# State-space stage: matrices fetched ahead, inputs one block later, another order of the gate matmuls

## What is computed

```python
u = (h @ w_in).reshape(B, S, G, C)          # 64 groups of 16 channels
# x[s] = a * x[s-1] + Bbar u[s], complex, 64 states a group
y = einsum('bsgp,gcp->bsgc', xr, c_re) - einsum('bsgp,gcp->bsgc', xi, c_im) + d_skip * u
y = gelu(y)
val, gate = split(y @ w_glu, 2)
h = h + val * sigmoid(gate)
```

## Time and profile before

| what | us |
|---|---|
| median of 3 runs | 1158.1 (1156.81 to 1161.51) |
| the profiled execution | 1160.05 |
| its span, first to last instruction | 1158.2 |
| PE busy | 1122.9 (97%) |
| DVE busy | 790.0 (68%) |
| ACT busy | 476.3 (41%) |
| POOL busy | 99.5 (9%) |

### The profile page before, as it was taken

One profiled execution on the slowest core, in us unless ns is written; L12 is line 12 of the kernel. 1 busy time (PEld: TensorE's weight loads), 2 busy tenths in 40 slices (PEclk: granted clock), 3 DMA queues, 4 the chain that ended last, 5 costly groups with the idle time before them and its releaser, 6 DMA issues.

```text
span 1158.2 us, 14812 instructions
## 1 busy us (share of the span) xinstructions
PE 1122.9 (97%) x5654; PEld 919.9 (79%) x5654; DVE 790.0 (68%) x1172; ACT 476.3 (41%) x718; POOL 99.5 (9%) x194
## 2 busy tenths in 40 slices
PE   9998999999999999999999979999999999999995
PEld 6776778788888888888778877887888888888874
DVE  6757758898776887678768855547764467635764
ACT  6455544345423543335452214334442244413431
POOL 3270008910000000000000000000000000000000
PEclk9999899899999999999999979999999999999998
DMA  6221103233343333433257853332232232233221
GB/s 225 87 69 37 37 19 109 74 109 111 110 137 117 109 128 103 134 110 123 97 173 216 234 162 108 94 108 91 92 104 96 91 101 100 91 99 102 82 82 72
DMA packets 61942, 125.68 MB, mean 109 GB/s; under 512 B 21808, under 2 KB 30512, under 8 KB 61872
## 3 DMA queue, kind: packets, MB, share of 16 engines
q1 hardware_dynamic: 60720, 120.54, 32.6%
q0 software_dynamic: 1152, 4.19, 1.0%
HBM read 110.04 MB, written 14.68 MB: 108 GB/s over the span
## 4 chain that ended last, share of the span: by engine, by line
PE 86%; DVE 6%; DMA 3%; issue 2%; ACT 2%; DVEq 1%; SPq 0%; ACTq 0%
PE bank L1418 27%; PE bank L1420 26%; PE bank L1419 26%; DMA ud_scratch<-UB 2%; DVE MX L1006 1%; DVE WL L812 1%; DVE P L1014 1%; PE bank L1745 1%; PE bank L1737 1%; ACT WH L477 1%; PE bank L1696 1%; PE bank L1437 1%; DMA yd_scratch<-Y 1%; DVEq L1005 1%; PE bank L1432 1%
## 5 line engine op out<-in xcount | busy, mean ns | idle before, releaser
L477 ACT ACTIVATE WH<-RAW 128x1024 fp32r<-128x1024 f32 (+1 forms) x184 | 190.1, 1034 | 387.7 <-PE bank L1420 367.8
L1418 PE MATMUL bank<-GH,WH 128*128 128x512 f32 x816 | 323.2, 396 | 4.2 <-DVE GL L1048 3.1
L1419 PE MATMUL bank<-GL,WH 128*128 128x512 f32 x816 | 318.8, 391 | 0.0
L1420 PE MATMUL bank<-GH,WL 128*128 128x512 f32 x816 | 318.7, 391 | 0.0
L812 DVE TENSOR_TENSOR WL<-RAW,WH 128x1024 fp32r<-128x1024 f32 (+1 forms) x184 | 221.2, 1203 | 46.9 <-ACT WH L477 46.2
L1418 PE MATMUL bank<-AH,WH 128*128 128x512 f32 x596 | 235.9, 396 | 2.7 <-DVE AL L1157 1.6
L1420 PE MATMUL bank<-AH,WL 128*128 128x512 f32 x596 | 232.9, 391 | 0.0
L1419 PE MATMUL bank<-AL,WH 128*128 128x512 f32 x596 | 232.7, 390 | 0.0
L1418 PEld LDWEIGHTS bank<-GH,WH 128*128 128x128 f32 x816 | 153.9, 189 | 38.9 <-DVE GL L1048 4.0
L1419 PEld LDWEIGHTS bank<-GL,WH 128*128 128x128 f32 x816 | 153.9, 189 | 32.8 <-issue 1.4
L1420 PEld LDWEIGHTS bank<-GH,WL 128*128 128x128 f32 x816 | 153.9, 189 | 32.6
(11 more groups left out here) (254 smaller groups left out, 997.0 us busy)
## 6 DMA issues: line engine op xcount, KB each, us to landing
RAW<-in_w_up SPq DMA_DIRECT2D x88, 512.0 KB, 3.4
RAW<-in_w_dn SPq DMA_DIRECT2D x32, 512.0 KB, 3.5
RAW<-in_w_glu SPq DMA_DIRECT2D x16, 512.0 KB, 3.6
RAW<-in_w_dn SPq DMA_DIRECT2D x16, 384.0 KB, 3.0
RAW<-in_w_wo SPq DMA_DIRECT2D x8, 512.0 KB, 3.5
od_scratch<-OO SPq DMA_DIRECT2D x8, 512.0 KB, 3.0
kd_scratch<-KT SPq DMA_DIRECT2D x8, 512.0 KB, 4.8
O<-od_scratch POOLq DMA_DIRECT2D x8, 512.0 KB, 5.3
```

What stands on the lines that cost most here:

```text
L477: act_(WH[b % RH][:, :n], RAW[b % RW][:, :n], ACT.Copy).then_inc(s_hi, 1)
L1418: mm(out, wh, hi_[:, k, :], start=start, stop=False)
L1419: mm(out, wh, lo_[:, k, :], start=False, stop=False)
L1420: return mm(out, wl, hi_[:, k, :], start=False, stop=stop)
```

## The change

TM and O get five places instead of two: tiles 0 and 4 lie in AH and AL at tiles 6 and 7, tile 3 in AH and AL at tiles 4 and 5, tile 7 where ET of tiles 0 and 1 was, tiles 1 and 5 and tiles 2 and 6 in the two old places. Tiles 0 to 3 are fetched before the stage's first waits, 4 to 7 during it, each when what lay in its place has been used. There is a fourth U buffer (over SQ1). Inputs and outputs come one block later: TensorE does block t, inputs(t - 3), outputs(t - 4), and VectorE and ScalarE follow. On SP the read of y stands behind the next u_out instead of behind its own write. The first three gate blocks all come behind the last outputs, in an order in which block 0 ends first, then 1, then 2.

```diff
+        matrices_at("_y6", ah_at + 6 * 4 * S, al_at + 6 * 4 * S, (0, 4))
+        matrices_at("_y4", ah_at + 4 * 4 * S, al_at + 4 * 4 * S, (3,))
+        matrices_at("_et", A0, A0 + 4096, (7,))
+        at = matrices_at("0", at, at + 4096, (1, 5))
+        at = matrices_at("1", at, at + 4096, (2, 6))
...
+        U2[3], _ = place("U23", [P, 2 * QJ, NK], F32, sq1_at)
...
+                if b == FIRST["dn02"] + 2:
+                    sp.wait_ge(s_mm, nth(FIRST["up02"] - 1))
+                    lags_in(0)
+                if b == FIRST["dn02"] + 4:
+                    sp.wait_ge(s_act, TILE0["h02"] + THIRDS[2][1])
+                    lags_in(1)
+                if b == FIRST["dn02"] + 6:
+                    lags_in(2)
...
             def u_in(j):
-                if j >= 3:
-                    sp.wait_ge(s_Y, j - 2)
+                if j >= 4:
+                    sp.wait_ge(s_Y, j - 3)
                 sp.wait_ge(s_uw, 16 * (j + 1))
...
-            for t in range(NJ + 3):
+            sp.wait_ge(s_mm, nth(FIRST["win"] - 1))
+            lags_in(3)
+            for t in range(NJ + 4):
                 if t < NJ:
                     load(FIRST["win"] + 4 + t)
                     u_out(t)
+                if 5 <= t <= NJ:
+                    y_in(t - 5)
+                if t < NJ:
                     u_in(t)
-                if t >= 3:
-                    y_out(t - 3)
-                    if t - 1 < NJ:
-                        lags_in(t - 1)
-                    y_in(t - 3)
+                if t == 5:
+                    sp.wait_ge(s_Y, 1)
+                    lags_in(4)
+                if t == 6:
+                    sp.wait_ge(s_Y, 2)
+                    lags_in(5)
+                    sp.wait_ge(s_E, 2)
+                    lags_in(7)
+                if t == 7:
+                    sp.wait_ge(s_Y, 3)
+                    lags_in(6)
+                if t >= 4:
+                    y_out(t - 4)
+                if t >= NJ:
+                    y_in(t - 4)
...
# VectorE (ScalarE likewise: gelu(t - 4), decay(t - 2), y_tile(t - 5))
-            for t in range(NJ + 4):
+            for t in range(NJ + 5):
                 if t < NJ:
                     u_out(t)
-                if 2 <= t < NJ + 2:
-                    states(t - 2)
-                if t >= 4:
-                    y_lo(t - 4)
+                if 3 <= t < NJ + 3:
+                    states(t - 3)
+                if t >= 5:
+                    y_lo(t - 5)
...
# POOL: fetch(0) and fetch(1) while the last third of the MLP runs, then
+            fetch(2)
+            pool.wait_ge(s_mm, nth(FIRST["win"] - 1))
+            fetch(3)
+            pool.wait_ge(s_Y, 1)
+            fetch(4)
+            pool.wait_ge(s_Y, 2)
+            fetch(5)
+            pool.wait_ge(s_E, 2)
+            fetch(7)
+            pool.wait_ge(s_Y, 3)
+            fetch(6)
...
# TensorE
             for t in range(2, NJ):
                 whole(FIRST["win"] + t, KD, GH, GL)
-                inputs(t - 2)
                 if t >= 3:
-                    outputs(t - 3)
-            inputs(NJ - 2)
-            outputs(NJ - 3)
-            inputs(NJ - 1)
-            outputs(NJ - 2)
-            glu_part((0, 1), range(0, 4))
+                    inputs(t - 3)
+                if t >= 4:
+                    outputs(t - 4)
+            for j in range(NJ - 3, NJ):
+                inputs(j)
+                outputs(j - 1)
             outputs(NJ - 1)
-            glu_part((0, 1), (4, 5))
-            glu_part((2,), range(0, 6))
-            glu_part((0, 1, 2), (6,))
-            glu_part((0, 1, 2), (7,))
+            glu_part((0,), range(0, 5))
+            glu_part((1,), range(0, 5))
+            glu_part((2,), range(0, 3))
+            glu_part((0, 1), (5,))
+            glu_part((2,), (3, 4))
+            glu_part((0,), (6, 7))
+            glu_part((1,), (6, 7))
+            glu_part((2,), range(5, 8))
```

More of the change, by code:

```diff
@@ L295, in build, with matrices_at @@
         KT, at = place("KT", [P, LQ, C * LQ], F32, at)
-        TM, O2, U2, XR, XI, UB, Y2, YB, RT = ([None, None] for _ in range(9))
-        U2 = [None] * 3
+        XR, XI, UB, Y2, YB, RT = ([None, None] for _ in range(6))
+        U2 = [None] * 4
+        TM, O2 = [None] * NJ, [None] * NJ
         at = f0
-        for i in range(2):
-            TM[i], at = place(f"TM{i}", [P, 2 * QJ, C * LQ], F32, at)
-            O2[i], at = place(f"O2{i}", [P, 2, QJ, C * LQ], F32, at)
+        ah_at, al_at = g_at + 2 * 4 * KD * S, g_at + 3 * 4 * KD * S
+        def matrices_at(name, tm_at, o_at, tiles):
+            tm, _ = place("TM" + name, [P, 2 * QJ, C * LQ], F32, tm_at)
+            o2, end = place("O2" + name, [P, 2, QJ, C * LQ], F32, o_at)
+            for j in tiles:
+                TM[j], O2[j] = tm, o2
+            return end
+        matrices_at("_y6", ah_at + 6 * 4 * S, al_at + 6 * 4 * S, (0, 4))
[3 more added lines that the diff above has]
+        at = matrices_at("1", at, at + 4096, (2, 6))
         for i in range(3):
             U2[i], at = place(f"U2{i}", [P, 2 * QJ, NK], F32, at)
+        U2[3], _ = place("U23", [P, 2 * QJ, NK], F32, sq1_at)
         for i in range(2):
@@ L344, in build @@
         s_kp, s_k0, s_kt, s_kw, s_ow = sem("KP"), sem("K0"), sem("KT"), sem("kd_written"), sem("od_written")
-        s_tmr, s_or = [sem("TM0"), sem("TM1")], [sem("O0"), sem("O1")]
-        s_uw, s_ur = sem("ud_written"), [sem(f"U{i}_loaded") for i in range(3)]
+        s_tmr = [sem(f"TM_of_tile{j}") for j in range(NJ)]
+        s_or = [sem(f"O_of_tile{j}") for j in range(NJ)]
+        s_uw, s_ur = sem("ud_written"), [sem(f"U{i}_loaded") for i in range(4)]
         s_rt, s_E, s_X, s_Y, s_g = sem("RT"), sem("E"), sem("states"), sem("Y"), sem("gelu")
@@ L402, in lags, with lags_in @@
                 sp.dma_start(KD_[j], KT[:]).then_inc(s_kw, 16)
+            def lags_in(j):
+                k = KD_[j]
+                sp.wait_ge(s_kw, 16 * (j + 1))
+                sp.dma_start(TM[j][:], bass.AP(k.tensor, k.offset, [[C * LQ, P], [C * LQ * P, GJ], [1, C * LQ]])
+                             ).then_inc(s_tmr[j], 16)
             for b in range(4, FIRST["win"] + 4):
@@ L782, in _ @@
                     hi(FIRST["win"] + t + RH)
[L783 to L786, removed]
-                if t >= 4:
-                    y_tile(t - 4)
+                if 4 <= t < NJ + 4:
+                    gelu(t - 4)
+                if 4 <= t < NJ + 2:
+                    decay(t - 2)
+                if t >= 5:
+                    y_tile(t - 5)
             for i in range(KD):
@@ L1399, in fetch @@
             def fetch(j):
-                if j >= 2:
-                    pool.wait_ge(s_Y, j - 1)
-                g.dma_start(O2[j % 2][:], OD[j].rearrange("p r (q n) -> p r q n", q=QJ)).then_inc(s_or[j % 2], 16)
+                pool.wait_ge(s_ow, 16 * (j + 1))
+                g.dma_start(O2[j][:], OD[j].rearrange("p r (q n) -> p r q n", q=QJ)).then_inc(s_or[j], 16)
+            pool.wait_ge(s_mm, nth(FIRST["up02"] - 1))
+            fetch(0)
+            pool.wait_ge(s_act, TILE0["h02"] + THIRDS[2][1])
+            fetch(1)
             pool.wait_ge(s_wcs, 1)
+            pool.wait_ge(s_et, NJ)
             pool.wait_ge(s_ow, 16 * NJ)
[L1406 to L1409, removed]
+            fetch(2)
[9 more added lines that the diff above has]
+            fetch(6)
         @block.tensor
@@ L1725, in inputs @@
                             c0 = (QJ * r + q) * NK
-                            m = mm(bank[2 + j % 2][rows, c0:c0 + NK], ET[:, j, r, q, rows], U2[j % 3][:, 2 * q + gi, :],
+                            m = mm(bank[2 + j % 2][rows, c0:c0 + NK], ET[:, j, r, q, rows], U2[j % 4][:, 2 * q + gi, :],
                                    start=True, stop=True)
@@ L1744, in outputs @@
                             rows = slice(64 * gi, 64 * gi + 64)
[L1745 removed]
+                            m = mm(bank[4 + 2 * p + gi][:, q * NK:(q + 1) * NK], O2[j][rows, r, q, :], x[p][rows, q, 0:NK],
                                    start=False, stop=(r == 1), skip_group_check=True)
```

20 lines of the change are left out of this document (6 added, 14 removed).

## The result

The changed kernel takes 1162.08 us (median of 15 runs, 1159.12 to 1165.52), the kernel before 1158.1 (15 runs, 1155.82 to 1161.8): a ratio of 1.0035, with a 95% interval of 1.0024 to 1.0047. It is 4 us slower, within the 0.5% that I called no change, and above the range of 1151.5 to 1161.5. The profiled execution took 1161.19 us, its span 1159.4, against 1160.05 before.

The account below looks back on a forecast made before the run. TensorE was taken to bound the kernel: -5.3 us at full clock, +2.1 and +2.1 for half clock, sum -1.1 us; taken from the median 1158.1, this gave 1157.0 us, range 1151.5 to 1161.5.

Parts of the forecast that it names:

- at full clock the stage is 5.3 us shorter: State-space stage: with the clock held, the fourth gate block starts at 703.6 against 708.87 before, 5.3 us earlier.
- The price of the clock: Stage's tail: half clock from O(6) costs 2.1 us until O(7) ends and 2.1 in the gate matmuls, together 4.2.
- last step, from one profile to the median: Whole kernel: the 1.1 us gain on the profiled 1160.05 us was taken from the median 1158.1 too, giving 1157.0.
- one at O(6) or O(7): Stage's tail, the forecast itself: clock falls late, at the wait for states(6) or states(7); 1157.0 us, chance 0.45.
- 4.9 us of work without a gap on either side: Argument against a clock fall at the 2.0 us wait for O(5): TensorE works 4.9 us without a gap around it.
- falls early: Rival: clock falls at the 2.0 us wait for O(5), TensorE then runs at half without waiting; 1157.7 us, chance 0.2.
- The y round trip: Stage's tail: y 3's write (median 3.6) and read (3.4) through DRAM hold VectorE's states(6) up by 1.6 us.
- the slower rival: Stage's tail: slow y round trips hold VectorE's chain; 1161.3 us with the longest landings of before, up to 1164.1; chance 0.12.
- the wait for U: TensorE ahead of tile 7's inputs: the 3.37 us wait goes because inputs come three blocks behind, with four U buffers.

Follow-up runs that it names:

- e8: The changed kernel with 13, 17 and 10 matmuls without use ahead of O(5), O(6) and O(7); median 1157.28 us, ratio to before 0.9964.
- e7: The changed kernel with the low halves of y 3, 4 and 5 one place later on VectorE; ratio to before 1.0048.
- e4: The changed kernel's homes, buffers and SP order, but the pipeline one block shorter and the gate order as before; ratio to before 0.9953.
- e2: The changed kernel with 9, 12 and 12 matmuls without use ahead of O(5), O(6) and O(7); ratio to before 1.0016.
- e1: The changed kernel with 24 gate matmuls back ahead of O(7); ratio to before 1.0008.
- e10: The new gate order in e4, so the changed kernel without the pipeline's lag of one block; ratio to before 0.9958.
- e3: The kernel before with 14 matmuls without use ahead of in(7) (inputs of tile 7) and 9 ahead of TM(6); ratio to before 0.9955.
- e6: e4 with useful gate matmuls put into the waits and gate blocks that end in turn; median 1148.25 us, ratio to before 0.9923.
- e9: The kernel before with the new gate order alone; ratio to before 1.0010.

## Why the prediction was wrong

It was 5.1 us too low (1162.08 against 1157.0). In my sum, -5.3 + 4.2 and then from the profile to the median, two steps failed.

The first is **"at full clock the stage is 5.3 us shorter"**. e8 is the changed kernel with its clock kept at 1.00 by matmuls without use, and its stage is 114.5 us, only 2.6 below the 117.1 that I started from. The term that was mis-sized is the time for which y holds VectorE: I put 1.6 us for y 3 and none for y 2, and it was 1.77 + 2.25 = 4.0 us in e8 and 2.9 to 4.3 in the changed kernel. States(7) so end 96.1 us into e8's stage, where I had 685.4 - 591.77 = 93.6. The price of the clock, 4.2 us in the sum, came out right (3.5 to 4.1), but with some luck: it was down for 23.9 us, not for the 15 that I forecast (678 to 693), partly while TensorE would have waited for VectorE anyway. The second is the **last step, from one profile to the median**, 2.8 us; it is the last term below.

The same difference, counted along the path that the changed kernel took (from the profiled executions, where I forecast -1.1 and +1.14 was measured):

- **Where the clock fell: 0.7 us.** I gave the fall at O(5) 0.2 and one at O(6) or O(7) 0.45. It fell at O(5), behind 2.31 us; e7 (2.55) shows the same. What failed is the argument "4.9 us of work without a gap on either side": waits of 1.76 (e4) and 1.14 us (the kernel before again) among these small matmuls, and one of 1.26 us behind twelve long ones (e2), were followed by half clock too. My rival "falls early" had the mechanism right, down to a TensorE that works on at half without waiting for states(7).
- **The sizes within that rival: 1.3 us.** It said 708.5 - 591.77 = 116.7 for the stage; 118.0 came. O(5) started 78.9 us into the stage, not 78.3: with y 2 late, a 0.46 us hold came that I had not counted. From there to the first gate matmul it took 691.25 - 671.07 = 20.2 (20.0 forecast), with 1.56 us of wait for states(6), held up by y 3, where I had none and some work still at full clock. The gate matmuls took 710.18 - 691.25 = 18.9, not 18.4, with 5.3 us at half for my 4.2.
- **The y round trip.** My 1.6 us of hold for y 3 were 2.46. The write took 5.7 us (6.2 and 7.3 in the other two profiles), where I took the median of all eight writes, 3.6. The row nearest to it was the write of y 4 beside TM(6), at 5.1, and my text named it. The rule of the Trainium skill (DMA: Bandwidth & Descriptors, Queues, rings and completion order) on descriptors of one ring agrees with the trace: the write of y 3, issued 0.6 us behind the load of TM(6), took longer than that of y 4 in before and landed 1.7 us behind TM(6) (0.8 us in the other two profiles). While TensorE is at half clock the hold costs little: without it, in e7, the stage is 0.4 to 1.0 us shorter. So the slower rival, held VectorE alone, isn't the path that the kernel took; but the hold is why the change has little to give at full clock.
- **Ahead of the stage and behind it: 0.4 and -0.2 us**, and the early loads of TM and O show no wait of their own there, as I took it.
- **From profile to median: 2.84 us.** I moved the 1.1 us from a profile that lay 1.95 above before's median; the changed kernel's profile lies 0.9 below its own. The five profiles of before show why one is a thin base: its DMA waits vary by 4.9 us. They don't close the account: before's stage is 116.6 on average and after's 118.3, 1.7 us apart, where the medians are 4.0 apart. Whether the waits were short in the runs that gave 1158.1, as in the profile of 113.7 us, can't be seen from unprofiled runs; some 2 us stay **open**. The same holds for e8, where ratios give 8 us and profiles 4. Before's own median moved from 1157.5 to 1160.81 us between the four occasions, and if part of that is its DMA waits, which the changed kernel does not have, it passes into every ratio; this isn't shown.

Above these is one that the total hides. I gave the longer pipeline the credit for the wait for U. In e4 that wait is gone without it, and the rows of SP and POOL put it down to the read of y 3, which no longer stands ahead of the write of u 7, and to the loads that no longer go beside that write. My account of the queue began at 664.35, with that write, and so missed what had held it up. What the longer pipeline does is to put a fourth states (5.7 us) behind the last win block. The change is thus a gain and a loss: homes, buffers and queue order alone give -5.4 us (0.9953). The longer pipeline then costs 6.4 us with gate matmuls ahead of O(7) (e4 to e1), or 8.9 by the ratio and about 4 by the stage without them (e10 to after). Moving the 24 gate matmuls away from O(7) adds 1.3 to 3.1 us (e1 to after).

Right were: no wait for U, TM or the weights; the last win block (VectorE takes its result at 655.53, for a forecast end of 655.0); VectorE as the chain that sets the pace until the clock falls; and that the DMA time lost in before would not come back whole. In e3 holding before's clock was worth 5.2 us by the ratio and 5.6 by the stage.

## What to carry to other kernels

Before lengthening a pipeline to hide a late load, ask whether the load is late by itself or only stands behind another step's wait in its queue, and count what the longer pipeline leaves for the next engine in its tail. In a stretch of small matmuls a wait of one or two microseconds can cost several at half clock; independent long matmuls belong into such waits rather than behind them (e6: 0.9923, against 1.0035 for the change as made). Where a kernel's waits on DMA vary, take the sum from several profiles, or keep their spread in the range.

## What the hardware did that I had not expected

- The clock fell from 2.4 to 1.2 GHz with waits of 1.14, 1.76 and 2.31 us among 64-column matmuls, and with one of 1.26 us in e2, behind twelve of 512 columns. The 1.25 us before O(5) in the same e2, behind nine of them, did nothing, so length alone doesn't decide. Nor is the fall always behind the wait: in e9 it came 0.6 us into a wait of 2.26 us, in e2 1.5 us after the wait had ended. With waits of 0.58 us and less, it stayed up (e6, e8).
- Once down, small matmuls didn't bring it back: in e7 it stayed down through 19 us of them without a gap (670.8 to 689.8). It came back 2.7 to 5.6 us after the 512-column matmuls of the gate had begun: 4.3 us in before and 5.3 in the changed kernel.
- The write of one y took 2.5 to 2.6 us where nothing else was under way, 5.7 to 7.3 behind one TM load (y 3), 5.5 to 6.7 behind two (y 2), and 8.3 to 8.8 behind a TM load with two O loads just ahead of it and a weight load behind it (y 1).
- The write of u 7 took 5.6 to 6.7 us in the five profiles of before, with the load of a weight block issued 0.5 us ahead of it and one of O 1.1 to 3.1 us behind it, and 3.1 to 4.0 in e4, e6 and e10, with the weight load 2.6 to 2.9 us ahead and no load of O.
